# Wider loads and alternating column pairs in the input projection of a decoder layer

## The chip, the cores and the metric

The kernel runs on one core of a Trainium2 chip. The metric is the time of one execution on the device in microseconds (us), taken as the median of several runs; lower is better. One execution was also profiled, and all rows below come from it.

## What is computed

One decoder layer for 256 tokens of width 2048, all in float32. An input projection w_in (2048 x 8208) gives queries, keys, values and output gates for two groups of 8 heads of 128, and 16 scalar gate columns. The first group is an mLSTM, the second a retention. Both mixers' results go through one output projection, then comes a feed-forward network.

```python
h = rmsnorm(x, g_mix_pre[l])
proj = h @ w_in[l]
mq, mk, mv, mo, mi, mf, rq, rk, rv, rg = jnp.split(proj, SPLITS, axis=-1)
qk = jax.nn.silu(causal_dwconv(jnp.concatenate([mq, mk], axis=-1), conv_w[l], conv_b[l]))
...
hm = head_rmsnorm(hm, g_mlstm_head[l]) * jax.nn.sigmoid(mo.astype(f32))
rq_h = rotary(split_heads(rq, N_RET_HEADS).astype(f32), positions)
rk_h = rotary(split_heads(rk, N_RET_HEADS).astype(f32), positions)
hr = retention_chunkwise(rq_h, rk_h, split_heads(rv, N_RET_HEADS).astype(f32))
hr = head_rmsnorm(hr, g_ret_head[l]) * jax.nn.silu(rg.astype(f32))
mix = jnp.concatenate([hm, hr], axis=-1).astype(x.dtype) @ w_out[l]
x = x + rmsnorm(mix, g_mix_post[l])
h = rmsnorm(x, g_ffn_pre[l])
ff = (jax.nn.silu(h @ w_gate[l]) * (h @ w_up[l])) @ w_down[l]
x = x + rmsnorm(ff, g_ffn_post[l])
```

## The kernel before

**Split products.** Each float32 operand is kept as two parts, a rounded one (`hi`) and the rest (`lo`), and a product is made of hi by hi, hi by lo and lo by hi. Weights pass through three stages. SyncE loads 1 MB chunks into `raw` (four chunks, q = 0 to 3). ScalarE copies 1024 columns of it, one **sub**, to `w_hi` (L441). VectorE writes the difference to `w_lo` (L779). `w_hi` and `w_lo` hold four subs (`AHEAD`), so ScalarE copies sub s + 4 as soon as TensorE has ended sub s (`ahead`), and VectorE follows. A chunk of `raw` serves two subs; `load` (L324) fills it again once `lo_done` says that both were used.

**Rounds.** Eight subs are a round. Rounds 0 to 3 make the values, rounds 4 to 15 (`R_IN` to `R_OUT`) the queries, keys and gates: for each of four head groups (two of the mLSTM, two of the retention) a query, a key and a gate round, each of 512 output columns. Rounds 16 to 19 are the output projection, then comes the feed-forward network. In rounds 4 to 15 a round makes two **pairs** (u = 0, 1) of 256 columns. Pair 0 takes subs 0 to 3, pair 1 subs 4 to 7 (`unit_columns`), each sub being 8 products of 512 and 8 of 256 moving columns (`sub_columns`). A load brings 8 rows of 256 columns per partition.

**After a pair.** `unit_at(rnd, s, lag)` says which pair ended `lag` subs ago. With lag 0, ScalarE copies the right half of the pair's two PSUM banks to `right` and VectorE adds the left half to it (`unit_sums`), which frees the banks (`acc_free`). Queries and keys then pass four convolution taps (`convolve`, half 0 at lag 0 and half 1 at lag 1) or the rotation (`rotate`), in the single buffer `new`, and at lag 2 ScalarE writes them to `qT` or `kT`. A gate's sums are scaled, and at lag 1 ScalarE applies the sigmoid (L604); in the retention groups VectorE multiplies at lag 2 by the gate itself (L1086).

**Heads.** The four heads n of a group are worked off from the start of its gate round. `head_at(rnd, s, first)` gives the head whose step falls on sub s. TensorE makes scores at s = 0, 2, 4, 6 and weighted values after s = 1, 3, 5, 7; the latter go to two PSUM banks in turn, so those of head n wait for `y_ready` of head n - 2. VectorE's `head_step` runs first in each step, in this order: `weigh` (head n at s = 2n), `mix` (2n + 6), `head_scaled` (2n + 4, which writes y), variance (2n + 3), reciprocals (2n + 2), `mix_rest` (2n + 8). `mix` (L1055) waits for `gate_sig`, the sigmoid of the head's pair. TensorE turns y of head 0 and 1 after subs 5 and 7, of heads 2 and 3 in the next round (`left_over`). Each engine runs its instructions in the written order.

**The scalar gates.** 16 products with `wg_both` fill bank 3, which is also a bank of pair 1. ScalarE copies parts of it to rows, VectorE combines them in short linked operations (L930 to L947), TensorE turns the result to columns (`gate_columns`), VectorE copies these (L956, L958), and `spread_rows` makes 16 products of 8 rows each for the decay matrices, after sub 0 of round 5.

Of the kernel before, what the change touches and what calls it, by code (L numbers as in the profile page):

```python
# [24 lines left out]
ALU = mybir.AluOpType  # L25
# [90 lines left out]

def unit_at(rnd, s, lag):

    rnd, s = rnd - (lag > s), (s - lag) % 8
    if R_IN <= rnd < R_OUT and s % 4 == 3:  # L120
        return (*divmod(rnd - R_IN, 3), s // 4)
    return None


def hybrid_layer(nc, x, positions, g_mix_pre, w_in, conv_w, conv_b, b_igate, b_fgate, g_mlstm_head,
                 g_ret_head, w_out, g_mix_post, g_ffn_pre, w_gate, w_up, w_down, g_ffn_post,
                 inv_freq, out):
    with ExitStack() as ctx:
# [86 lines left out]

        def acc(pair):
            return bank[:, 2 * pair:2 * pair + 2, :]
# [45 lines left out]
        gates_act = sem("gates_act")  # L263
        gates_dve = sem("gates_dve")
# [53 lines left out]
        def _(sp):  # L318
            def load(rnd, q, src, wait=True):

                if wait:
                    sp.wait_ge(lo_done, 8 * (rnd - 1) + 2 * q + 2)
# [106 lines left out]
        def _(act):  # L429
# [4 lines left out]
            def hi(rnd, s, first=False):  # L434
# [3 lines left out]
                rnd, s = rnd + s // 8, s % 8  # L438
                if not first:
                    act.wait_ge(raw_full[s // 2], 16 * (rnd + 1))  # L440
                act.activation(w_hi[:, s % AHEAD, :], raw[:, s // 2, (s % 2) * SUB:(s % 2 + 1) * SUB],  # L441
                               ACT.Copy).then_inc(hi_done, 1)
# [151 lines left out]
            def mixer_step(rnd, s):  # L594

                ended = unit_at(rnd, s, 0)
# [3 lines left out]
                if ended and ended[1] == 2:  # L600
# [3 lines left out]
                    act.activation(new if group >= 2 else gT[:, two, :], gT[:, two, :], ACT.Sigmoid)\  # L604
                       .then_inc(gate_sig, 1)
                ended = unit_at(rnd, s, 2)
                if ended and ended[1] < 2:
                    group, part, u = ended
                    act.wait_ge(tiles_done, pair_of(group, part, u) + 1)
                    act.activation((qT, kT)[part][:, 2 * u:2 * u + 2, :], new,  # L610
                                   ACT.Silu if group < 2 else ACT.Copy).then_inc(pair_ready, 1)

            def gate_rows():
# [6 lines left out]
                act.wait_ge(gates_dve, 3)  # L620
# [145 lines left out]
        def _(dve):  # L766
# [8 lines left out]
            def lo(rnd, s):  # L775
# [3 lines left out]
                dve.tensor_tensor(w_lo[:, s % AHEAD, :], raw[:, s // 2, (s % 2) * SUB:(s % 2 + 1) * SUB],  # L779
                                  w_hi[:, s % AHEAD, :].bitcast(F32), ALU.subtract).then_inc(lo_done, 1)  # L780
# [147 lines left out]
            for n, p0 in enumerate((0, 32)):  # L928
                z = row(R_Z)[p0:p0 + HEADS]
                link(dve.scalar_tensor_tensor(z, row(R_LEFT_LO)[p0:p0 + HEADS], 1.0,  # L930
                                              row(R_RIGHT_LO)[p0:p0 + HEADS], ALU.mult, ALU.add))
                link(dve.tensor_tensor(z, z, row(R_RIGHT)[p0:p0 + HEADS], ALU.add))
                link(dve.tensor_tensor(z, z, bank[p0:p0 + HEADS, B_GATES, 0:SEQ], ALU.add))
                link(dve.tensor_tensor(z, z, rstd_row[p0:p0 + HEADS, :], ALU.mult))
                gates(dve.tensor_scalar(z, z, vec[p0:p0 + HEADS, 2:3], None, ALU.add), n + 1)
            gates(dve.scalar_tensor_tensor(rowf(R_ABS), rowf(R_Z), -1.0, rowf(R_Z), ALU.mult, ALU.max), 3)
# [135 lines left out]
            def mixer_step(rnd, s):  # L1072
# [9 lines left out]
                ended = unit_at(rnd, s, 2)  # L1082
                if ended and ended[0] >= 2 and ended[1] == 2:
                    group, part, u = ended
# [165 lines left out]
        def _(pe):  # L1250
# [12 lines left out]
            def sub_columns(rnd, s, act_T, pair):  # L1263

                pe.wait_ge(lo_done, 8 * rnd + s + 1)
                slot, quarter = s % AHEAD, s % 4
# [9 lines left out]
            def unit_columns(rnd, unit, event, act_T, before=None, after=None):  # L1276

                pe.wait_ge(acc_free, event + 1)
                for q in range(4):
# [3 lines left out]
                    sub_columns(rnd, s, act_T, unit)  # L1283
# [173 lines left out]
            def gate_units(group, rnd, event):  # L1457
# [11 lines left out]
                for u in range(2):  # L1469
                    unit_columns(rnd, u, event + u, hT, before, after)  # L1470
# [5 lines left out]
            unit_columns(R_IN, 0, event_of(R_IN, 0), hT)  # L1476
            pe.wait_ge(gates_act, 1)
            pe.wait_ge(gates_dve, 2)
            unit_columns(R_IN, 1, event_of(R_IN, 1), hT,
                         after=lambda s: gate_columns() if s == 6 else None)  # L1480
            for u in range(2):
                unit_columns(R_IN + 1, u, event_of(R_IN + 1, u), hT,
                             after=lambda s: spread_rows() if s == 0 else None)
            with pe.Fori(0, 3) as j:
                gate_units(j, 3 * j + gate_round(0), 6 * j + event_of(gate_round(0), 0))
                for n in (1, 2):
                    for u in range(2):
                        unit_columns(3 * j + (gate_round(0) + n), u,
                                     6 * j + event_of(gate_round(0) + n, u), hT,
                                     after=left_over(j) if n == 1 else None)  # L1490
# [121 lines left out]
```

## Time and profile before

| | |
|---|---|
| median of 3 timed runs | 1235.89 us (1235.27 to 1236.32) |
| the profiled execution | 1238.89 us |
| its span, first to last instruction | 1237.2 us |
| granted TensorE clock, mean | 0.996 |
| TensorE busy | 1222.7 us |
| VectorE busy | 717.1 us |
| ScalarE busy | 599.3 us |
| loads of w_in, 63 of 1 MB, issue to landing | 12.8 us (median) |

Rows name an engine (PE is TensorE, DVE VectorE, ACT ScalarE, PEld the weight load of TensorE, SP SyncE), a line of the kernel, what is written and read, and times. Times on a timeline count from the start of the span. Matmuls overlap, so a start-to-start distance tells more of TensorE's pace than one duration does.

### The profile page before, as it was taken

How to read it: one execution, taken by the hardware profiler on the slowest of the kernel's cores; microseconds unless marked ns; L12 is line 12 of the kernel's file. 1: busy time of each engine (PE TensorE's matmuls, PEld its weight loads, DVE VectorE, ACT ScalarE, POOL GpSimd, SP SyncE). 2: the span in 40 equal slices, each digit the busy share in tenths (PEclk: the TensorE clock that was granted, in tenths of full speed). 3: DMA queues.
4: the chain of work that ended last, by engine and by line, in shares of the span. 5: the costliest groups of instructions: out<-in, count | busy, mean ns of one | idle time of the engine just before them, and what ended most of it. 6: DMA issues, size and time to landing. Idle time of an engine off the chain costs nothing.

```text
span 1237.2 us, 15798 instructions
## 1 busy us (share of the span) xinstructions
PE 1222.7 (99%) x5899; PEld 1026.1 (83%) x5899; DVE 717.1 (58%) x923; ACT 599.3 (48%) x789; POOL 14.2 (1%) x35
## 2 busy tenths in 40 slices
PE   8999999999999999999999999999999999999997
PEld 7888888888888888888888888888888888888886
DVE  6656778776777656744554554454455454544544
ACT  5654666574554645644444444444444444443442
POOL 2000100000000000000000000000000000000000
PEclk9999899999999999999999999999999999999999
DMA  8666798867887556465656565555656565556551
GB/s 313 208 145 165 132 213 171 146 166 163 204 179 187 200 178 214 157 193 181 194 180 203 175 198 190 183 192 184 200 173 200 188 220 203 182 192 204 186 188 69
DMA packets 136937, 229.49 MB, mean 185 GB/s; under 512 B 6080, under 2 KB 55488, under 8 KB 136384
## 3 DMA queue, kind: packets, MB, share of 16 engines
q1 hardware_dynamic: 136608, 226.84, 62.8%
q0 software_dynamic: 288, 2.10, 0.4%
q8 instruction: 26, 0.43, 0.1%
q14 instruction: 15, 0.12, 0.0%
HBM read 226.83 MB, written 2.10 MB: 185 GB/s over the span
## 4 chain that ended last, share of the span: by engine, by line
PE 90%; DMA 4%; DVE 3%; ACT 1%; issue 0%; SPq 0%; DVEq 0%; ACTq 0%
PE bank L1252 89%; DMA raw<-in_w_in 4%; DVE w_lo L779 1%; PE bank L1536 1%; DMA resid<-in_x 1%; ACT w_hi L441 1%; PE bank L1257 0%; PE bank L1454 0%; DVE gT L993 0%; ACT L604 0%; DVE h L806 0%; DVE resid L1124 0%; PE bank L1509 0%; DVE pre L966 0%; DVE hT L792 0%
## 5 line engine op out<-in xcount | busy, mean ns | idle before, releaser
L779 DVE TENSOR_TENSOR w_lo<-raw,w_hi 128x1024 fp32r<-128x1024 f32 x420 | 512.9, 1224 | 481.8 <-ACT w_hi L441 481.3
L441 ACT ACTIVATE w_hi<-raw 128x1024 fp32r<-128x1024 f32 x420 | 443.5, 1060 | 569.4 <-PE bank L1252 539.1
L1252 PE MATMUL bank<-w_hi,h2T 128*128 128x512 f32 x1376 | 426.6, 390 | 0.0
L1252 PEld LDWEIGHTS bank<-w_hi,h2T 128*128 128x128 f32 x1376 | 258.3, 188 | 53.4
L1252 PE MATMUL bank<-hT,w_hi 128*128 128x512 f32 x768 | 274.5, 401 | 0.0
L1252 PE MATMUL bank<-w_lo,h2T 128*128 128x512 f32 x688 | 267.7, 389 | 0.0
L1252 PE MATMUL bank<-w_hi,ffT 128*128 128x512 f32 x704 | 217.2, 389 | 0.0
L1252 PE MATMUL bank<-hT,w_lo 128*128 128x256 f32 x768 | 215.4, 280 | 0.0
L1252 PEld LDWEIGHTS bank<-hT,w_hi 128*128 128x128 f32 x768 | 145.5, 190 | 33.8 <-issue 0.2
L1252 PEld LDWEIGHTS bank<-w_hi,ffT 128*128 128x128 f32 x704 | 132.1, 188 | 27.3
L1252 PEld LDWEIGHTS bank<-w_lo,h2T 128*128 128x128 f32 x688 | 129.2, 188 | 26.5
L1252 PEld LDWEIGHTS bank<-hT,w_lo 128*128 128x128 f32 x768 | 146.1, 190 | 0.0
L1252 PE MATMUL bank<-w_lo,ffT 128*128 128x512 f32 x352 | 136.9, 389 | 0.0
L1252 PE MATMUL bank<-w_hi,hT 128*128 128x512 f32 x256 | 81.3, 393 | 0.8 <-DVE w_lo L779 0.8
L1252 PE MATMUL bank<-w_hi,mixT 128*128 128x512 f32 x256 | 80.2, 391 | 0.0
L1252 PEld LDWEIGHTS bank<-w_lo,ffT 128*128 128x128 f32 x352 | 66.1, 188 | 13.8
L1252 PEld LDWEIGHTS bank<-w_hi,hT 128*128 128x128 f32 x256 | 48.0, 188 | 11.3 <-issue 1.2
L1252 PEld LDWEIGHTS bank<-w_hi,mixT 128*128 128x128 f32 x256 | 48.1, 188 | 10.3 <-DVE mixT L1061 0.4
L1252 PE MATMUL bank<-w_lo,hT 128*128 128x512 f32 x128 | 49.9, 390 | 0.0
L1252 PE MATMUL bank<-w_lo,mixT 128*128 128x512 f32 x128 | 49.8, 389 | 0.0
L1252 PEld LDWEIGHTS bank<-w_lo,mixT 128*128 128x128 f32 x128 | 24.0, 188 | 4.9
L1252 PEld LDWEIGHTS bank<-w_lo,hT 128*128 128x128 f32 x128 | 24.1, 188 | 4.7
(176 smaller groups left out, 566.4 us busy)
## 6 DMA issues: line engine op xcount, KB each, us to landing
raw<-in_w_in SPq DMA_DIRECT2D x63, 1024.0 KB, 12.8
raw<-in_w_gate SPq DMA_DIRECT2D x44, 1024.0 KB, 5.1
raw<-in_w_up SPq DMA_DIRECT2D x44, 1024.0 KB, 5.1
raw<-in_w_down SPq DMA_DIRECT2D x44, 1024.0 KB, 5.0
raw<-in_w_out SPq DMA_DIRECT2D x16, 1024.0 KB, 5.0
resid<-in_x SPq DMA_DIRECT2D x2, 1024.0 KB, 7.2
out<-resid SPq DMA_DIRECT2D x8, 256.0 KB, 2.5
raw<-in_w_in SPq DMA_DIRECT2D x2, 512.0 KB, 6.6
```

Of the source, the lines that this page charges most:

```text
L441: act.activation(w_hi[:, s % AHEAD, :], raw[:, s // 2, (s % 2) * SUB:(s % 2 + 1) * SUB], ACT.Copy).then_inc(hi_done, 1)
L779: dve.tensor_tensor(w_lo[:, s % AHEAD, :], raw[:, s // 2, (s % 2) * SUB:(s % 2 + 1) * SUB], w_hi[:, s % AHEAD, :].bitcast(F32), ALU.subtra ...
L1252: return pe.matmul(out_, lhsT, rhs, start=start, stop=stop, skip_group_check=True)
L1536: ins = pe.transpose(bank[:, B_FF + j // 2, c:c + P], ff[:, t, j * P:(j + 1) * P], ident)
```

## The change

Loads of rounds 4 to 15 bring 4 rows of 512 columns per partition, so that each chunk serves both pairs. The order of the subs of a round becomes a table of (pair, chunk). In query and gate rounds (`EVEN_ORDER`) the pairs alternate by two subs: pair 0 ends with sub 5, pair 1 with sub 7. In key rounds (`KEY_ORDER`) pair 0 ends with sub 4. `free_after` gives the count at which a chunk may be overwritten. On ScalarE the activation of a query or key pair moves ahead of the copy of the right half. The gates of the retention groups use one SiLU in place of sigmoid and product. The scalar gates read bank 3 first, and the forget row goes ahead of the input row.

```diff
+EVEN_ORDER = ((0, 0), (0, 1), (1, 0), (1, 1), (0, 2), (0, 3), (1, 2), (1, 3))
+KEY_ORDER = ((0, 0), (0, 1), (1, 0), (0, 2), (0, 3), (1, 1), (1, 2), (1, 3))
+ORDERS = (EVEN_ORDER, KEY_ORDER, EVEN_ORDER)
+FREE = (2, 4, 6, 8)
...
+def free_after(part):
+
+    return [ORDERS[part].index((1, q)) + 1 for q in range(4)]
...
-    if R_IN <= rnd < R_OUT and s % 4 == 3:
-        return (*divmod(rnd - R_IN, 3), s // 4)
+    if R_IN <= rnd < R_OUT:
+        ends = [ORDERS[(rnd - R_IN) % 3].index((u, 3)) for u in range(2)]
+        if s in ends:
+            return (*divmod(rnd - R_IN, 3), ends.index(s))
...
+        def raw_sub(rnd, s):
+
+            if is_wide(rnd):
+                u, q = ORDERS[(rnd - R_IN) % 3][s]
+                return q, raw[:, q, :].rearrange("p (k c) -> p k c", c=512)[:, :, 256 * u:256 * u + 256]
+            return s // 2, raw[:, s // 2, (s % 2) * SUB:(s % 2 + 1) * SUB]
...
-                            col = COL_RET * kind + 512 * half + (part * DH + (q // 2) * 256)
-                            load(6 * kind + 3 * half + (R_IN + n), q,
-                                 in_rows(8 * (q % 2), 8, col, 256))
-            with sp.Fori(0, 4) as g:
+                            col = COL_RET * kind + 512 * half + part * DH
+                            load(6 * kind + 3 * half + (R_IN + n), q, in_rows(4 * q, 4, col, 512),
+                                 free=free_after((n + 2) % 3))
+            for q in range(4):
+                load(R_OUT, q, rows(w_out, 4 * q, 4, 0, 512), free=free_after(2))
+            with sp.Fori(1, 4) as g:
...
+                ended = unit_at(rnd, s, 2)
+                if ended and ended[1] < 2:
+                    group, part, u = ended
+                    act.wait_ge(tiles_done, pair_of(group, part, u) + 1)
+                    act.activation((qT, kT)[part][:, 2 * u:2 * u + 2, :], new,
+                                   ACT.Silu if group < 2 else ACT.Copy).then_inc(pair_ready, 1)
...
-                    act.activation(new if group >= 2 else gT[:, two, :], gT[:, two, :], ACT.Sigmoid)\
+                    act.activation(gT[:, two, :], gT[:, two, :], ACT.Silu if group >= 2 else ACT.Sigmoid)\
                        .then_inc(gate_sig, 1)
...
-            for n, p0 in enumerate((0, 32)):
+            for p0 in (0, 32):
+                dve.tensor_tensor(row(R_Z)[p0:p0 + HEADS], bank[p0:p0 + HEADS, B_GATES, 0:SEQ],
+                                  row(R_RIGHT)[p0:p0 + HEADS], ALU.add).then_inc(gates_left, 1)
+            dve.wait_ge(gates_left, 2)
+            for n, p0 in enumerate((32, 0)):
...
-                    dve.wait_ge(gate_sig, 2 * group + u + 1)
-                    link(dve.tensor_tensor(gT[:, 2 * u:2 * u + 2, :], gT[:, 2 * u:2 * u + 2, :], new,
-                                           ALU.mult))
...
+            def wide_columns(rnd, event, act_T, order, before=None, after=None):
+
+                for s, (u, q) in enumerate(order):
+                    if q == 0:
+                        pe.wait_ge(acc_free, event + (u + 1))
...
+            def gates_consumed(s):
+
+                if s == 2:
+                    pe.wait_ge(gates_act, 1)
+                    pe.wait_ge(gates_left, 2)
```

What stands in a row on ScalarE around the first gate activation of the first group's gate round, before. The first w_hi copy is sub 3's step, the second sub 4's step:

```order
L441 ACTIVATE w_hi<-raw 128x1024 [waits raw_full3,sub_done]
L561 ACTIVATE right<-bank 128x512 [waits acc_free]
L457 ACT_TABLE_LOAD
L457 ACTIVATE stat<-stat 128x2 [waits var_ready]
L588 ACTIVATE stat<-bank 128x2 [waits pv_done]
L441 ACTIVATE w_hi<-raw 128x1024 [waits raw_full0,sub_done]
L604 ACT_TABLE_LOAD
L604 ACTIVATE gT<-gT 128x512 [waits gate_scaled]
```

And there now, where the first w_hi copy is sub 5's step and the second sub 6's step:

```order
L475 ACTIVATE w_hi<-raw 128x1024 [waits raw_full1,sub_done]
L594 ACTIVATE right<-bank 128x512 [waits acc_free]
L490 ACTIVATE stat<-stat 128x2 [waits var_ready]
L621 ACTIVATE stat<-bank 128x2 [waits pv_done]
L475 ACTIVATE w_hi<-raw 128x1024 [waits raw_full0,sub_done]
L643 ACT_TABLE_LOAD
L643 ACTIVATE gT<-gT 128x512 [waits gate_scaled]
```

The gate activation has moved two steps down, behind the copy that waits for sub 6. On VectorE, steps 5 and 6 of the same round, before (`stat` rows are the heads' statistics, L1055 is `mix`, L1047 writes y):

```order
L779 TENSOR_TENSOR w_lo<-raw,w_hi 128x1024 [waits hi_done]
L1021 SCALAR_TENSOR_TENSOR probs<-bank,decay 128x384 [waits pv_done,masked,scores_done]
L1055 SCALAR_TENSOR_TENSOR gT<-bank,columns,gT 128x256 [waits gate_sig,yT_done]
L1041 RECIPROCAL stat<-stat 128x2 [waits sd_ready]
L1042 TENSOR_TENSOR stat<-stat 128x2 [waits dve_step]
L1047 TENSOR_SCALAR y<-bank,stat 128x128 [waits dve_step]
L1047 TENSOR_SCALAR y<-bank,stat 128x128
```

And now, where L1091 is `mix` and L1083 writes y:

```order
L812 TENSOR_TENSOR w_lo<-raw,w_hi 128x1024 [waits hi_done]
L1002 TENSOR_TENSOR gT<-bank,right 128x512 [waits right_ready]
L1005 TENSOR_TENSOR gT<-gT,rstd_row 128x512 [waits acc_free]
L1057 SCALAR_TENSOR_TENSOR probs<-bank,decay 128x384 [waits pv_done,masked,scores_done]
L1091 SCALAR_TENSOR_TENSOR gT<-bank,columns,gT 128x256 [waits gate_sig,yT_done]
L1077 RECIPROCAL stat<-stat 128x2 [waits sd_ready]
L1078 TENSOR_TENSOR stat<-stat 128x2 [waits dve_step]
L1083 TENSOR_SCALAR y<-bank,stat 128x128 [waits dve_step]
L1083 TENSOR_SCALAR y<-bank,stat 128x128
```

The first pair's sums and scaling now stand directly ahead of step 6, and `mix` keeps its place ahead of y. The third place is VectorE's start of the scalar gates, now (before, ten linked operations stood ahead of the absolute value):

```order
L962 TENSOR_TENSOR h0<-bank,h0 8x256 [waits gates_act,rope_ready]
L962 TENSOR_TENSOR h0<-bank,h0 8x256
L968 TENSOR_TENSOR h0<-h0 8x256 [waits gates_left]
L968 TENSOR_TENSOR h0<-h0 8x256 [waits dve_step]
L969 TENSOR_TENSOR h0<-h0,rstd_row 8x256 [waits dve_step]
L970 TENSOR_SCALAR h0<-h0,vec 8x256 [waits dve_step]
L972 SCALAR_TENSOR_TENSOR h0<-h0 8x256 [waits gates_dve]
```

The absolute value (L972) has six operations ahead of it, and the bank is read by the first two.

## Rows read from the trace of the kernel before

**Rows 1.** The page: TensorE's busy time, and the chain by engine.

```profile
PE 1222.7 (99%) x5899; PEld 1026.1 (83%) x5899; DVE 717.1 (58%) x923; ACT 599.3 (48%) x789; POOL 14.2 (1%) x35
...
PE 90%; DMA 4%; DVE 3%; ACT 1%; issue 0%; SPq 0%; DVEq 0%; ACTq 0%
```

**Rows 2.** Waits of TensorE, 106 to 422 us; last row: 410 to 425 us.

```profile
PE bank L1252 <- DVE probs L1021: 1.7, 1, 1.7
PE bank L1252 <- DVE floor L958: 0.8, 1, 0.8
PE bank L1252 <- ACT kT L610: 0.6, 1, 0.6
PE bank L1454 <- DVE y L1047: 0.2, 1, 0.2
...
PEld bank L1454 <- DVE y L1047: 0.5, 1, 0.5
```

**Rows 3.** Windows: busy by engine (count), granted clock, DMA share, GB/s.

```profile
134.50:136.00 1.50, 1.50 (x8) 1.18 (x7) 1.43 (x4) 0.00 (x0) 0.00 (x0) 0.54 0.85 117
136.00:141.00 5.00, 5.00 (x17) 4.32 (x16) 3.60 (x8) 0.07 (x1) 0.00 (x0) 0.50 0.90 97
141.00:143.00 2.00, 2.00 (x11) 1.70 (x11) 0.98 (x1) 1.51 (x2) 0.00 (x0) 0.89 0.61 91
...
304.00:314.00 10.00, 7.79 (x46) 6.40 (x45) 6.98 (x9) 4.16 (x6) 0.00 (x0) 1.00 0.86 230
```

**Rows 4.** Loads: w_in from 30, from 78, w_out; ScalarE's wait (106 to 380).

```profile
raw<-in_w_in SPq DMA_DIRECT2D x7, 1024.0 KB, 7.0
...
DMA to landing us min/median/max: 7.6/13.6/22.4
...
raw<-in_w_out SPq DMA_DIRECT2D x16, 1024.0 KB, 5.0
...
ACT w_hi L441 <- DMA raw<-in_w_in: 23.3, 7, 6.0
```

**Rows 5.** ScalarE's timeline, first gate round: start, duration, what, idle before.

```profile
175.47 1.06 ACT L441 ACTIVATE w_hi<-raw 128x1024 fp32r<-128x1024 f32 x1 [0.98 <-PE bank L1252]
176.55 1.28 ACT L604 ACT_TABLE_LOAD   x1
177.84 0.63 ACT L604 ACTIVATE gT<-gT 128x512 f32<-128x512 f32 x1
...
182.56 1.06 ACT L441 ACTIVATE w_hi<-raw 128x1024 fp32r<-128x1024 f32 x1 [0.73 <-PE bank L1252]
...
185.34 1.06 ACT L441 ACTIVATE w_hi<-raw 128x1024 fp32r<-128x1024 f32 x1 [0.49 <-PE bank L1252]
...
189.00 1.06 ACT L441 ACTIVATE w_hi<-raw 128x1024 fp32r<-128x1024 f32 x1 [1.97 <-PE bank L1252]
```

**Rows 6.** Timeline at the scalar gates (VectorE) and the row spread (TensorE).

```profile
107.96 0.40 DVE L930 SCALAR_TENSOR_TENSOR h<-h 8x256 f32<-8x256 f32 x1
...
131.95 0.28 PE L1252 MATMUL bank<-hT,w_lo 128*128 128x256 f32 x1
133.00 2.47 PE L1252 MATMUL bank<-neg_m,sel_r 8*128 8x256 f32 x16 [0.77 <-DVE floor L958]
```

**Rows 7.** VectorE's timeline in the first gate round; L1086 in all.

```profile
181.90 0.48 DVE L1055 SCALAR_TENSOR_TENSOR gT<-bank,columns,gT 128x256 f32<-128x256 f32 x1
...
182.68 0.61 DVE L1047 TENSOR_SCALAR y<-bank,stat 128x128 f32<-128x128 f32 x2
...
196.05 0.61 DVE L1047 TENSOR_SCALAR y<-bank,stat 128x128 f32<-128x128 f32 x2
...
L1086 DVE TENSOR_TENSOR gT<-gT,pre x4: 684/684/686, 330.6 to 418.4; 128x512 f32<-128x512 f32 x4
```

**Rows 8.** TensorE's timeline, first group: weighted values and turned y of head 3.

```profile
185.14 0.83 PE L1252 MATMUL bank<-v_sb,probs 128*128 x6
...
197.35 0.38 PE L1454 MATMUL bank<-columns,y 128*128 128x128 f32 x2
```

More of the change, by code:

```diff
@@ L318, in _, with load @@
         def _(sp):
-            def load(rnd, q, src, wait=True):
+            def load(rnd, q, src, wait=True, free=FREE):
                 if wait:
-                    sp.wait_ge(lo_done, 8 * (rnd - 1) + 2 * q + 2)
+                    sp.wait_ge(lo_done, 8 * (rnd - 1) + free[q])
                 k = src.shape[1]
@@ L438, in hi @@
                 rnd, s = rnd + s // 8, s % 8
+                chunk, src = raw_sub(rnd, s)
                 if not first:
-                    act.wait_ge(raw_full[s // 2], 16 * (rnd + 1))
-                act.activation(w_hi[:, s % AHEAD, :], raw[:, s // 2, (s % 2) * SUB:(s % 2 + 1) * SUB],
-                               ACT.Copy).then_inc(hi_done, 1)
+                    act.wait_ge(raw_full[chunk], 16 * (rnd + 1))
+                act.activation(part_of(w_hi, rnd, s), src, ACT.Copy).then_inc(hi_done, 1)
             def early_hi(s):
@@ L778, in lo @@
                 dve.wait_ge(hi_done, 8 * rnd + s + 1)
-                dve.tensor_tensor(w_lo[:, s % AHEAD, :], raw[:, s // 2, (s % 2) * SUB:(s % 2 + 1) * SUB],
-                                  w_hi[:, s % AHEAD, :].bitcast(F32), ALU.subtract).then_inc(lo_done, 1)
+                dve.tensor_tensor(part_of(w_lo, rnd, s), raw_sub(rnd, s)[1],
+                                  part_of(w_hi, rnd, s).bitcast(F32), ALU.subtract).then_inc(lo_done, 1)
             def early_lo(s):
@@ L927, in _ @@
             dve.wait_ge(gates_act, 1)
-            for n, p0 in enumerate((0, 32)):
+            for p0 in (0, 32):
[3 more added lines that the diff above has]
+            for n, p0 in enumerate((32, 0)):
                 z = row(R_Z)[p0:p0 + HEADS]
[L930 to L933, printed above, removed]
+                for lower in (R_LEFT_LO, R_RIGHT_LO):
+                    link(dve.tensor_tensor(z, z, row(lower)[p0:p0 + HEADS], ALU.add))
                 link(dve.tensor_tensor(z, z, rstd_row[p0:p0 + HEADS, :], ALU.mult))
-                gates(dve.tensor_scalar(z, z, vec[p0:p0 + HEADS, 2:3], None, ALU.add), n + 1)
-            gates(dve.scalar_tensor_tensor(rowf(R_ABS), rowf(R_Z), -1.0, rowf(R_Z), ALU.mult, ALU.max), 3)
+                gates(dve.tensor_scalar(z, z, vec[p0:p0 + HEADS, 2:3], None, ALU.add), 2 * n + 1)
+                if n == 0:
+                    gates(dve.scalar_tensor_tensor(rowf(R_ABS), rowf(R_Z), -1.0, rowf(R_Z), ALU.mult, ALU.max), 2)
             link(dve.memset(rowf(R_ONES), 1.0))
@@ L1261, in transposed, with sub_columns @@
                     ins.then_inc(xT_done, 1)
[L1263 removed]
+            def sub_columns(rnd, s, act_T, pair, quarter):
                 pe.wait_ge(lo_done, 8 * rnd + s + 1)
[L1266 removed]
+                slot = s % AHEAD
                 for c in range(2):
@@ L1282, in unit_columns @@
                         before(s)
-                    sub_columns(rnd, s, act_T, unit)
+                    sub_columns(rnd, s, act_T, unit, q)
+                    if after:
+                        after(s)
+            def wide_columns(rnd, event, act_T, order, before=None, after=None):
+                for s, (u, q) in enumerate(order):
+                    if q == 0:
+                        pe.wait_ge(acc_free, event + (u + 1))
+                    if before:
+                        before(s)
+                    sub_columns(rnd, s, act_T, u, q)
                     if after:
```

39 lines of the change are left out of this document (15 added, 24 removed).

## The prediction

> **What bounds the kernel now.** I read the page first: TensorE is busy 99% of the span, and 90% of the chain that ended last is TensorE [rows 1]. So only three things move the time: products added or removed, clock lost, and idle time of TensorE. The change adds and removes no product. Therefore the next view is TensorE's waits in the input projection (106 to 422 us): 1.7, 0.8, 0.6 and 0.2 us, four waits in all [rows 2]. The clock by windows shows the rest: it is 0.54 from 134.5 us and 0.50 from 136, and comes back within the window from 141 (0.89) [rows 3]. Time at the half level is about 6.8 us (92% of 1.5 us, 5 us, and 22% of 2 us), so 3.4 us are lost. All that the change can win is thus 3.3 us of waits, 0.2 us in the last gate round (below), and 3.4 us of clock: 6.9 us of 1236. Anything larger has to come as a loss.
>
> **Part 1: wider loads.** 48 loads of 1 KB runs become 48 loads of 2 KB runs of the same 1 MB. Now they land in 13.6 us in the median, 22.4 us at most, while the 512-column loads of w_out, of the very shape that w_in's now get, land in 5.0 us, and the 1024-column loads of w_in itself in 7.0 us [rows 4]. I take 5 to 9 us, nearest to these two, and keep 13.6 us as the upper bound. ScalarE waited 23.3 us for such loads in this stage, 7 times [rows 4]; three of TensorE's waits hang on that: the key activation (0.6 us), the weighted scores (1.7 us) and the turned head (0.2 us) [rows 2]. They go: -2.5 us. Another of this kind, a turned head in the last gate round (0.5 us of the weight load's wait [rows 2], of which the matmul row shows 0.2 us), also goes, since the SiLU now needs no product on VectorE (0.69 us [rows 7]) ahead of it: -0.2 us.
>
> The Trainium skill (Perfetto Trace Analysis, DMA Optimizations) says that transfers under 2 KB carry much overhead per transfer and that batching can improve throughput dramatically. Taken as the main effect it would promise far more, but here TensorE waits 2.7 us in all behind those loads, so the trace caps the gain whatever the bandwidth does.
>
> The other side of it: a chunk is now free later. In the key round chunk 1 is released after the sixth sub and wanted by the second of the next round: three subs instead of six. A sub is 2.78 us (the two w_hi copies at 182.56 and 185.34 [rows 5]), and the counts stand for a copy that follows its release by 3 x 2.78 plus 0.5 us, 8.8 us. TensorE uses the sub three later, less 2.3 us for w_hi and w_lo, so it has 6.0 us more, 14.8 us. The upper bound of 13.6 us fits for TensorE, not for ScalarE. I cost it at nothing; the cover is those 6.0 us.
>
> **Part 2: the gates' start and the row spread.** TensorE's wait for the gates' bank moves from the fifth to the third sub, 5.6 us after the round's start at 106.8. VectorE starts on them at 107.96, and an operation there takes 0.40 us [rows 6]; two additions free the bank at 108.8, against 112.3. No cost. The forget row then comes first: its absolute value follows 6 operations instead of 10, 4 x 0.44 = 1.8 us earlier, and with it everything down to the columns. The first query pair ends two subs later, but still ahead of the columns, so VectorE has the same work before them. I follow it by durations: sub 5 ends at 106.8 + 6 x 2.78 = 123.5, the copy behind it at 124.7, then on VectorE w_lo to 125.9, sums, norm and taps 2.9, w_lo 1.1, taps 1.6, columns 0.2: 131.8 us, where TensorE got them shortly before 133.00 now [rows 6]. TensorE is there at 132.2 (last product's start 131.95 plus 0.28). Its wait of 0.8 us [rows 2, 6] goes: -0.8 us. The cover is 0.4 us thin; if it fails, up to 0.8 us stays.
>
> Whether the clock still falls is open. It fell about 2.3 us after the dense products ended, within the 16 products of 8 rows, which took 2.5 us themselves [rows 3, 6]. These stay; only 0.8 us of idle time goes. Bounds: 0 and -3.4 us. I take 0, since the spread alone is as long as the stretch after which the clock fell.
>
> **Part 3: the gate round, where the change costs.** Before, the first pair of a gate round ends with sub 3 and ScalarE makes its sigmoid behind the w_hi copy of sub 4: copy 175.47, table 176.55, sigmoid 177.84 to 178.47, so 3.00 us from copy to end [rows 5]. VectorE multiplies with it in step 6 (L1055), without a wait, and in the same step makes y of head 1: 181.90 to 183.29, 1.39 us [rows 7]. TensorE wants y of head 1 (its PSUM bank) before the fourth weighted product, at 185.14 [rows 8], 1.85 us later. Now the pair ends with sub 5, the sigmoid stands in ScalarE's step 6, behind a copy that waits for sub 6, and VectorE's step 6 still multiplies first. So the multiplication waits: copy 182.56 [rows 5] + 3.00 = 185.56, + 1.39 = 186.95, + 0.1 for two hand-overs = 187.05, against 185.14. TensorE stands still for 1.9 us. Nothing gives it back, since TensorE has no other idle time. Queued behind the waiting multiplication are y, the reciprocals of head 2, and w_lo of sub 10; behind these ScalarE's squares and the next two copies. w_lo of sub 10 ends at 188.5 and is used from 193.5, covered. The turned heads are not quite: y of head 2 is then ready at about 193.6 where TensorE, itself 1.9 us later, comes at 193.5; y of head 3, 7.7 us (189.00 to 196.66) behind its step's copy, at 199.5 against 199.4 [rows 5, 7, 8]. That is 0 to 0.8 us more, I take 0.15. There are four gate rounds: 4 x (1.9 + 0.15) = +8.2 us.
>
> One price inside this differs from the Trainium skill (ScalarE: Activation LUTs, What ACT_TABLE_LOAD costs): 1.28 us for the load plus 1.38 us of drain for each switch. The row agrees with the load; the activation starts 0.01 us after it ends (176.55 + 1.28, then 177.84 [rows 5]). The measurement decides; with the page's drain the sum would be 4 x 1.4 us higher.
>
> **The rest of the pairs.** The second pair now ends two subs (5.6 us) before its banks are wanted again, instead of four. In a query round ScalarE must first take the first pair's activation: taps end about 2.8 us after the last sub, activation 0.6, copy of the right half 0.6, sum 0.7: 4.75 us. Covered by 0.8 us; nothing. Copies and differences read raw in four pieces of 256: the same sizes, no cost.
>
> **Sum**, against this execution's own 1238.9 us (span 1237.2): -2.7 - 0.8 + 8.2 = +4.7 us, 1243.6 us. The median of the timed runs lies 3.0 us under the profiled one, so 1235.9 + 4.7 = **1240.6 us**.
>
> **Rivals.** (a) The clock holds through the spread. For it: 0.8 us less without dense products. Against: the 2.5 us of thin ones. It takes off 3.4 us: 1237.2 us, 0.1% slower. (b) The faster side: the sigmoid does not reach TensorE. The place is the wait of L1055's product for gate_sig in step 6; it decides at 1.85 us between y of head 1 and the weighted product [rows 7, 8]. If the sigmoid were ready by 184, through an order of the engines that I misread, only the gains are left: 1235.9 - 3.5 = 1232.4 us, or 1229.0 with the clock kept. Against it: in the order both engines' rows stand as told, and the copy before the table load waits for sub 6. (c) The clock falls at the new 1.9 us gaps as well. Before, the wait of 1.7 us [rows 2] left it at 1.00 (the window from 304) [rows 3]; the new gap is longer. One fall costs the 3.4 us above: 1244.0 us with one, 1254.2 us with four. (d) Loads stay at 13 us or more and the short spans after key rounds reach ScalarE's copies in the gate rounds: the three waits of part 1 stay, +2.7, and about 1 us more: 1244.3 us. (e) That the loads are not wider is out: the order shows 128x4x512.
>
> **Chances.** Forecast 0.46, (a) 0.27, (b) 0.10, (c) 0.12, (d) 0.05. About 0.2% (2.5 us) is what a measurement of this kernel can tell from no change. Faster by more: (b), 0.10. Within: (a), 0.27. Slower: forecast, (c) and (d), 0.63. The range takes in the forecast with its bounds (0.8 us for the columns, up to 0.6 us a gate round), (a), (d) and (c) with one fall: 1234.5 to 1246.0 us; outside are (b) and most of the rest of (c).
>
> **What would show it.** In the profile after: a wait of TensorE for y or, at the fourth weighted product, of about 1.9 us, four times; VectorE's gate product waiting for the sigmoid's line on ScalarE four times, about 3 us each; no wait for the floor columns; w_in landings at 5 to 9 us and no ScalarE wait for them; the clock by windows near 134 us. The prediction is wrong if TensorE's waits in the gate rounds sum to under 4 us, if the clock falls more than once, or if the loads land no sooner.

## The result, and the profile after

| | before | after |
|---|---|---|
| median of 7 timed runs | 1235.89 us (1235.27 to 1237.51) | 1244.73 us (1242.16 to 1249.26) |
| ratio | | 1.0074 (95%: 1.0056 to 1.0093) |
| the profiled execution | 1238.89 us | 1242.16 us |
| its span | 1237.2 us | 1240.5 us |

The change makes the kernel 0.74% slower: 8.8 us, where 4.7 us were forecast. The page of the profile after still shows a kernel bound by TensorE [rows 1], now with less of it busy:

```profile
PE 1219.0 (98%) x5899; PEld 1023.9 (83%) x5899; DVE 715.0 (58%) x919; ACT 600.4 (48%) x789; POOL 13.2 (1%) x35
```

The waits from 106 to 422 us (engine, line, who was waited for: total, times, longest), which answer to [rows 2] and the last row of [rows 4]:

```profile
DVE gT L1091 <- ACT gT L643: 13.4, 4, 3.4
...
PE bank L1282 <- DVE y L1083: 7.9, 4, 2.0
ACT w_hi L475 <- DMA raw<-in_w_in: 3.8, 2, 2.0
...
PE bank L1282 <- ACT kT L633: 2.1, 2, 1.8
```

The three waits behind loads and the one for the floor columns are gone. In their place TensorE waits 7.9 us for `y`, four times, and 2.1 us for `kT`, twice. The first of the four, on the timelines of ScalarE, VectorE and TensorE (start, duration, what, idle time before), to be held against [rows 5, 7, 8]:

```profile
177.90 0.16 ACT L621 ACTIVATE stat<-bank 128x2 f32<-128x2 f32 x1
180.73 1.06 ACT L475 ACTIVATE w_hi<-raw 128x1024 fp32r<-128x1024 f32 x1 [2.67 <-PE bank L1282]
181.81 1.28 ACT L643 ACT_TABLE_LOAD   x1
183.10 0.63 ACT L643 ACTIVATE gT<-gT 128x512 f32<-128x512 f32 x1
```

```profile
183.84 0.48 DVE L1091 SCALAR_TENSOR_TENSOR gT<-bank,columns,gT 128x256 f32<-128x256 f32 x1 [3.37 <-ACT gT L643]
...
184.63 0.61 DVE L1083 TENSOR_SCALAR y<-bank,stat 128x128 f32<-128x128 f32 x2
```

```profile
185.49 0.93 PE L1282 MATMUL bank<-v_sb,probs 128*128 x6 [1.97 <-DVE y L1083]
```

ScalarE idles for 2.67 us until sub 6 has ended, then copies, loads the table, and makes the sigmoid; VectorE stands 3.37 us before the gate product, with `y` queued behind it, and TensorE 1.97 us before the weighted values. The other new wait is at the start of the first group's gate round (TensorE, then ScalarE, then VectorE):

```profile
156.00 0.92 PE L1282 MATMUL bank<-qT,kT 128*128 128x256 f32 x4 [1.78 <-ACT kT L633]
```

```profile
152.52 1.28 ACT L633 ACT_TABLE_LOAD   x1
155.32 0.63 ACT L633 ACTIVATE kT<-pre 128x512 f32<-128x512 f32 x1 [1.52 <-DVE pre L1029]
```

```profile
152.47 1.23 DVE L812 TENSOR_TENSOR w_lo<-raw,w_hi 128x1024 fp32r<-128x1024 f32 x1
153.61 0.88 DVE L1029 SCALAR_TENSOR_TENSOR gT<-pre,columns,gT 128x256 f32<-128x256 f32 x2
154.40 0.88 DVE L1029 SCALAR_TENSOR_TENSOR pre<-pre,columns,gT 128x256 f32<-128x256 f32 x2
```

The key pair that now ends with sub 4 of the key round instead of sub 3 passes its taps behind a `w_lo`, and the scores want it at 154.2 us. At the row spread (timeline of TensorE, against [rows 6]) there is no idle time, and the clock, by a window as in [rows 3], stays at the full level through the whole stretch:

```profile
132.07 2.17 PE L1282 MATMUL bank<-neg_m,sel_r 8*128 8x256 f32 x16
```

```profile
106.00:425.00 319.00, 308.96 (x1803) 270.57 (x1802) 236.62 (x417) 188.07 (x305) 5.81 (x17) 1.00 0.65 168
```

The loads of w_in from 78 us on (against [rows 4]) land in 9.0 us instead of 13.6:

```profile
DMA to landing us min/median/max: 5.9/9.0/14.2
```

**The account.** The profiled execution before lost 3.4 us to the clock at 134 us, the one after nothing there. So, held at the full clock, the two stand at 1235.5 and 1242.2 us: +6.7 us. The rows give +7.9 (`y`) + 2.1 (`kT`) - 0.8 (floor) - 2.5 (waits behind loads) = +6.7 us. That it closes so well is in part luck. A wait costs more than the idle time listed for it: from the first `w_hi` product of a round to that of the next, the four gate rounds last 118.8 us here and 109.7 us in e11 below, which has no waits for `y`. That is 9.0 us for a listed 7.9. Small differences in the pace of the products (see e1) stand against it.

The medians differ by 8.8 us, 2.1 us more. The median after lies 2.6 us above its profiled execution, that of before 0.4 us above the 1235.5 us worked out for the full clock. The mean granted clock is 0.998 in the profiled execution after and 0.993 to 0.997 in the four slowest timed runs. The experiments bear on what that is.

### The profile page after: what moved, and what is told of

The parts are those of the page before. It is cut to its first block, busy times and chain, and to the rows that moved or that the text cites. A ratio compares the mean times of both kernels' runs of the same rounds, so it can differ in the third digit from the quotient of the medians.

```text
span 1240.5 us, 15775 instructions
## 1 busy us (share of the span) xinstructions
PE 1219.0 (98%) x5899; PEld 1023.9 (83%) x5899; DVE 715.0 (58%) x919; ACT 600.4 (48%) x789; POOL 13.2 (1%) x35
## 4 chain that ended last, share of the span: by engine, by line
PE 94%; DVE 2%; ACT 2%; DMA 1%; issue 0%; SPq 0%; DVEq 0%
PE bank L1282 93%; PE bank L1577 1%; DMA resid<-in_x 1%; ACT w_hi L475 1%; DVE w_lo L812 1%; ACT L643 0%; PE bank L1287 0%; PE bank L1495 0%; DVE gT L1029 0%; ACT gT L643 0%; DVE y L1083 0%; ACT decay L587 0%; DVE h L839 0%; DVE resid L1154 0%; PE bank L1550 0%
## 5 line engine op out<-in xcount | busy, mean ns | idle before, releaser
L1282 PE MATMUL bank<-hT,w_hi 128*128 128x512 f32 x768 | 271.2, 397 | 0.0
L1282 PEld LDWEIGHTS bank<-w_lo,ffT 128*128 128x128 f32 x352 | 66.1, 188 | 13.6
```

The costliest lines, as they stand in the source:

```text
L1282: return pe.matmul(out_, lhsT, rhs, start=start, stop=stop, skip_group_check=True)
```

## The experiments

Each kernel ran in five rounds beside the kernel before, whose medians were 1236.09 us (first four rows below), 1236.48 us (next four) and 1236.13 us (last two).

| kernel | median (range), us | ratio to before (95%) |
|---|---|---|
| e1_y_first | 1241.49 (1240.27 to 1244.14) | 1.0050 (1.0036 to 1.0064) |
| e3_late_sigmoid | 1244.65 (1243.39 to 1251.81) | 1.0081 (1.0059 to 1.0103) |
| e4_narrow | 1246.21 (1244.72 to 1249.36) | 1.0086 (1.0072 to 1.0101) |
| e8_filled | 1243.08 (1242.18 to 1245.15) | 1.0060 (1.0047 to 1.0073) |
| e2_gate_early | 1237.11 (1234.70 to 1238.36) | 0.9997 (0.9986 to 1.0008) |
| e9_both | 1235.02 (1233.47 to 1237.61) | 0.9987 (0.9976 to 0.9997) |
| e5_input_row_first | 1246.68 (1244.20 to 1249.33) | 1.0077 (1.0057 to 1.0097) |
| e7_gates_only | 1234.37 (1233.24 to 1240.31) | 0.9981 (0.9964 to 0.9997) |
| e11_sig_ahead | 1233.72 (1233.14 to 1235.43) | 0.9980 (0.9972 to 0.9989) |
| e12_sig_and_taps | 1232.14 (1231.43 to 1233.60) | 0.9967 (0.9956 to 0.9978) |

The theory: the late sigmoid makes the four waits for `y` and with them most of the loss. The rivals: the loss comes from the loads or the order of subs itself, or from the clock.

### The late sigmoid in the old kernel (e3)

The kernel before, with the first gate pair's activation two steps later; retention gates use one SiLU, as after.

```diff
-                ended = unit_at(rnd, s, 1)
-                if ended and ended[1] == 2:
+                ended = unit_at(rnd, s, 3 if s == 6 else 1)
+                if ended and ended[1] == 2 and s != 4:
...
```

> The kernel before with its own loads, its own order of pairs and its own scalar gates, but the activation of the first gate pair is put two steps later on ScalarE, behind the copy of sub 10 (retention gates with one SiLU, as in the change, because the second product would stand in the way). Theory: TensorE waits for y four times, 1.9 us each, so +7.7 us, less 0.2 us for the SiLU: 1243 us where the clock holds, and a spread of several us above it, as in the changed kernel. Rival 1 (loads or interleaving): within 1 us of the kernel before, 1236 us.

Its waits, and windows around one place:

```profile
DVE gT L1055 <- ACT gT L604: 18.7, 4, 4.7
PE bank L1246 <- DVE y L1047: 8.0, 4, 2.0
```

```profile
262.00:263.00 1.00, 0.81 (x7) 0.82 (x8) 0.97 (x2) 0.73 (x4) 0.00 (x0) 1.00 0.67 188
263.00:266.50 3.50, 3.50 (x15) 3.02 (x13) 2.40 (x5) 3.47 (x8) 0.00 (x0) 0.52 0.38 89
```

The same four waits, 8.0 us, without any of the change's loads or orders, and 8.6 us more time than before. The mechanism stands. The windows show something more: directly behind the second of the four gaps the granted clock is at 1.2 GHz for about 3.4 us, which costs 1.7 us. The clock is not all that varies: the slowest run (1251.81 us) has the same mean clock, 0.996, as the three runs between 1243.4 and 1244.8 us. What it lost is not known.

### y ahead of the gate product (e1)

```diff
-                for step, first in ((weigh, 0), (mix, 6), (head_scaled, 4), (head_variance, 3),
+                for step, first in ((weigh, 0), (head_scaled, 4), (mix, 6), (head_variance, 3),
```

> The changed kernel, but VectorE's head step writes y (L1083) ahead of the product with the gate (L1091); nothing else moves. Theory (the late gate activation holds y of head 1, and through it TensorE): the four waits of about 2.0 us before the fourth weighted product go, and at most 0.3 us each is left before the turned head behind it, since that needs the gate product of head 0. The wait for keys (2.1 us) stays. With no 2 us gaps left the clock should fall no more there, so the runs lie close together: about 1235 us in the median, spread under 2 us. Rival 1 (wider loads or the interleaved pairs themselves cost): still 1240 us or more. Rival 2 (the clock falls for another reason, such as the row spread): the median falls by 7 us only and the spread of 7 us stays.

It missed by 6 us, and by its own terms it spoke for rival 1 (loads or pairs, 1240 us or more), which e3 speaks against and e11 below refutes. TensorE no longer waits for `y` before the weighted values, but for the gate product before the turned heads, at 106 to 425 us:

```profile
PE bank L1495 <- DVE gT L1091: 2.9, 9, 0.5
...
PE bank L1282 <- ACT kT L633: 2.0, 2, 1.8
```

Of 7.9 us 5.0 are saved by the waits, yet the span is only 1.2 us shorter (1239.3 us). The starts of the rounds say where the rest is. The four gate rounds are 6.8 us shorter in all. The stretches behind them, in which heads 2 and 3 are turned (three query rounds and the output projection), are 4.3 us longer, and the three key rounds from the second group on 1.1 us longer. Two things make that up. A late turned head costs more than its listed wait. In the changed kernel it starts 0.12 us after the product before it, here 0.55 us, for a listed 0.27:

```profile
191.91 0.28 PE L1282 MATMUL bank<-hT,w_lo 128*128 128x256 f32 x1
192.03 0.38 PE L1495 MATMUL bank<-columns,y 128*128 128x128 f32 x2
```

```profile
190.41 0.28 PE L1282 MATMUL bank<-hT,w_lo 128*128 128x256 f32 x1
190.96 0.41 PE L1495 MATMUL bank<-columns,y 128*128 128x128 f32 x2 [0.27 <-DVE gT L1091]
```

Over all turned heads these distances are 4.8 us longer than in the changed kernel, for 2.9 us of listed waits. The other is the pace of the products. A sub that nothing interrupts takes 2.77 us in some stretches and 2.83 us in others, all at the full clock: of 41 such subs 35 are slow here and 5 in the changed kernel, which is 1.7 us. Windows of 20 us of nearly the same stretch, in the changed kernel and here, show it as 118 products against 115:

```profile
281.00:301.00 20.00, 20.00 (x118) 1.00 0.71 171
```

```profile
281.00:301.00 20.00, 20.00 (x115) 1.00 0.70 173
```

e11, which differs from the changed kernel in one instruction of ScalarE, also has 115 there, and 15 slow subs in all. What sets the pace was not found.

### Narrow loads under the new order (e4)

The changed kernel with loads of 8 rows of 256 columns. The order and the ends of the pairs are kept; the counts at which a chunk may be overwritten change with the layout.

```diff
-                            col = COL_RET * kind + 512 * half + part * DH
-                            load(6 * kind + 3 * half + (R_IN + n), q, in_rows(4 * q, 4, col, 512),
+                            col = COL_RET * kind + 512 * half + (part * DH + (q % 2) * 256)
+                            load(6 * kind + 3 * half + (R_IN + n), q, in_rows(8 * (q // 2), 8, col, 256),
...
```

> The changed kernel with its order of pairs, its activations and its scalar gates, but with loads of 8 rows of 256 columns as before, laid out so that a chunk serves two subs of one pair. Theory: the y waits stay (7.9 us); loads take 13 us again, so ScalarE waits for them some 20 us in all, and the 0.6 to 2.5 us that TensorE lost through them come back: 1243 to 1247 us. Rival 1 (the wide loads are what costs, through the shorter spans for a chunk): 1238 us or less. If the wide loads gave nothing: as the changed kernel within 1 us, with no more waits of TensorE in its profile.

```profile
ACT w_hi L476 <- DMA raw<-in_w_in: 11.2, 4, 3.7
PE bank L1283 <- DVE y L1084: 8.8, 4, 2.9
...
PE bank L1283 <- ACT kT L634: 2.1, 2, 1.8
```

The loads of w_in land in 11.8 us instead of 9.0 (medians of the two pages), and ScalarE waits 11.2 us for them, where some 20 were expected. One wait for `y` grows to 2.9 us, in the round in which ScalarE waits 3.19 us for a load at 259 us. The waits account for 0.9 us more than in the changed kernel. The other 3.4 us of this profile are two falls of the clock, one at the row spread (135 us) and one behind the wait of 2.9 us (264.8 us). The median lies 1.5 us above the changed kernel's, with intervals of the ratios that overlap, so what the wide loads are worth under this order is not settled by the times. The loss itself stays with narrow loads: it is not theirs.

### The gaps filled with work (e8)

The changed kernel plus 8 products of 512 columns, extra work into bank 0, before the fourth weighted values of each gate round.

```diff
+                        if s == 7:
+                            pe.wait_ge(acc_free, event + 3)
+                            for _ in range(8):
+                                mm(bank[:, 0, :], hT[:, 0, 0:P], hT[:, 0, :], True, True)
```

> The changed kernel with eight products of 512 columns added on TensorE in each gate round between sub 7 and the fourth weighted product, about 1.8 us, in the time in which it stands still; their result is overwritten. Theory (the clock falls in the idle gaps, in some executions): the lowest time stays at 1242 us, because the gap is only filled, and the spread goes: median within 1 us of the lowest, and the mean granted clock the same in all runs. Rival 2 (the clock falls elsewhere): the spread of 7 us stays and the median stays at 1244 to 1245 us.

```profile
PE bank L1282 <- ACT kT L633: 2.0, 2, 1.8
PE bank L1282 <- DVE y L1083: 0.2, 1, 0.2
```

```profile
156.00:157.00 1.00, 0.78 (x4) 0.72 (x5) 0.64 (x1) 1.00 (x2) 0.00 (x0) 0.87 0.86 207
157.00:160.00 3.00, 3.00 (x11) 2.61 (x11) 2.78 (x4) 0.60 (x2) 0.00 (x0) 0.50 0.89 183
```

The idle time became work of the same length, and the fastest run is the same to 0.02 us (1242.18). But the runs spread over 3.0 us instead of 7.1, and the median is 1.65 us lower. These are six runs against seven, and the intervals of the two ratios overlap, so this supports, and does not prove, that the clock falling behind the gaps lifts the changed kernel's median over its fastest run. The fall that this profile holds stands right behind the one long gap that was not filled, that for `kT` (1.8 us). The mean clock was expected to be the same in all runs; it is 0.996 to 0.999.

### The gate pair ends one sub sooner (e2)

```diff
-ORDERS = (EVEN_ORDER, KEY_ORDER, EVEN_ORDER)
+ORDERS = (EVEN_ORDER, KEY_ORDER, KEY_ORDER)
...
-                wide_columns(rnd, event, hT, EVEN_ORDER, before, after)
+                wide_columns(rnd, event, hT, KEY_ORDER, before, after)
```

> The changed kernel with one table entry changed: gate rounds run in KEY_ORDER, so that the first gate pair ends with sub 4 instead of sub 5 and its sigmoid stands one step earlier on ScalarE. Theory (the sigmoid's place sets the four 2.0 us waits for y): the gate product on VectorE finds the sigmoid ready (at about 181.3 us in the first gate round, where it is wanted at 181.9), TensorE's waits for y go from 7.9 us to under 1 us, without the waits of the turned heads that the other order of the head step had; span 1240.5 - 7.9 = 1232.6 to 1234 us, and no clock falls at gate gaps. Rival (a second link, such as VectorE's load with the sums of both pairs, is late next): over 3 us of waits stay at the weighted or turned products, and the span is 1237 us or more.

```profile
ACT w_hi L475 <- DMA raw<-in_w_in: 14.8, 7, 3.0
...
PE bank L1282 <- ACT kT L633: 2.1, 2, 1.8
DVE gT L1091 <- ACT gT L643: 1.3, 4, 0.3
PE bank L1282 <- DVE probs L1057: 1.2, 1, 1.2
```

All 7.9 us for `y` are gone, and the time is that of the kernel before. The span, 1235.4 us, is over the 1232.6 to 1234 us expected: 1240.5 - 7.9 = 1232.6 us, plus 1.2 us for `probs` and 1.7 us for one fall of the clock at the row spread, makes 1235.5. The price is visible: chunk 1 is free later in the gate rounds too, ScalarE waits 14.8 us for loads instead of 3.8, and once that reaches TensorE (1.2 us).

### The keys' taps first (e9)

As e2, and in VectorE's loop, for step 5 of a key round:

```diff
+                    taps_first = (rnd - R_IN) % 3 == 1 and s == 5
+                    if taps_first:
+                        mixer_step(rnd, s)
                     lo(rnd, s + AHEAD)
-                    mixer_step(rnd, s)
+                    if not taps_first:
+                        mixer_step(rnd, s)
```

> The kernel with gate rounds in KEY_ORDER, and in step 5 of a key round VectorE finishes the first pair's taps before it makes w_lo of the sub ahead. Theory (TensorE's 2.1 us of waits for kT at the start of the gate rounds hang on VectorE's taps, which end at 155.28 us behind a w_lo of 1.14 us): the key activation ends 1.1 us sooner, the waits of 1.78 and 0.37 us shrink to 0.7 and 0 us; span 1.5 us under that of the kernel with gate rounds in KEY_ORDER alone. Rival (w_lo of sub 9 becomes late, or the activation is held by ScalarE's table load): the same waits of about 2 us stay, or show at w_lo instead.

```profile
PE bank L1286 <- DVE probs L1057: 1.8, 1, 1.8
...
PE bank L1286 <- ACT kT L633: 0.6, 1, 0.6
```

The waits for `kT` fall from 2.1 to 0.6 us, as told, and the span from 1235.4 to 1234.0 us. The wait behind the loads stays (1.8 us). The clock fell in both profiles at the row spread, though nothing waits there; in this one:

```profile
134.50:137.90 3.40, 3.40 (x13) 2.92 (x12) 3.37 (x8) 1.06 (x1) 0.00 (x0) 0.52 0.67 175
```

### The scalar gates (e5, e7)

e5 is the changed kernel with the input row first again and the absolute value behind both rows; e7 is the kernel before with only the scalar gates' new code.

```diff
-            for n, p0 in enumerate((32, 0)):
+            for n, p0 in enumerate((0, 32)):
...
```

> The changed kernel with the scalar gates in the old order of rows: input row first, and the absolute value behind both rows. Theory (the forget row first brings the columns 1.8 us sooner and takes the 0.8 us wait at the row spread away): a wait of TensorE of 0.5 to 1.8 us for floor or cols stands at 131 to 133 us again, span 1241 to 1242.5 us where the clock holds; a clock fall at the spread, if the idle time there decides it, adds up to 3.4 us. Rival (the columns were no longer late because the first query pair ends later, whatever the row order): no wait, the same time as the changed kernel, 1242 to 1245 us.

> The kernel before with only the scalar gates' part of the change: bank 3 read first, forget row first, absolute value after six operations. Theory: the columns are ready 1.8 us sooner, the wait of 0.8 us for the floor columns before the row spread goes, nothing else moves: 0.8 us less, so about 1235 us, and 1233.1 us where the clock holds. If the fall of the clock at 134 us in the profile before came from that 0.8 us of idle time, it is absent here in every run; if it comes from the 16 products of 8 rows alone, it still shows in some runs (3.4 us more). Rival: the columns are late behind the first query pair's taps, not behind the gates' operations, and nothing changes.

The waits of e5:

```profile
PE bank L1282 <- ACT kT L633: 3.1, 2, 2.8
...
PE bank L1282 <- DVE floor L994: 0.2, 1, 0.2
```

The row order alone is worth 0.2 us at the spread, less than the 0.5 expected, and 1.0 us at `kT`: the decay exponentials start later on ScalarE and hold up the copy of the key pair's right half (from 149.48 us, against 148.16). The profile's span is 1246.5 us, 6.0 us above the changed kernel's: 1.2 us of waits, and three falls of the clock (at 158.0, 188.7 and 267.2 us) of 1.7 us each, each beginning 0.3 to 1.2 us after the end of a wait, those for `kT` and for the first two `y`. In e7 the columns are copied at 130.78 and 130.86 us, against 132.61 and 132.69 us before, and the spread follows without a wait:

```profile
130.78 0.17 DVE L960 COPY a_col<-bank 128x16 f32<-128x16 f32 x1
130.86 0.16 DVE L962 COPY floor<-bank 128x16 f32<-128x16 f32 x1
```

```profile
132.14 1.58 PE L1256 MATMUL bank<-neg_m,sel_r 8*128 8x256 f32 x11
```

So this part alone is worth 1.8 us on the columns and the 0.8 us of wait; the median is 2.1 us lower, with an interval of the ratio that means 0.4 to 4.5 us. Its profiled execution (1240.31 us) also shows how much the old loads vary from one execution to the next:

```profile
PE bank L1256 <- DVE probs L1025: 5.3, 2, 2.8
```

```profile
164.00:168.00 4.00, 4.00 (x16) 3.45 (x15) 3.54 (x9) 0.69 (x2) 0.00 (x0) 0.57 0.72 192
```

Two waits behind loads of up to 2.8 us, and behind each a clock fall. That the slow executions of the kernel before (up to 1244.98 us, mean clock 0.992) come from the same is likely and not shown.

### The sigmoid ahead of the copy (e11, e12)

The order of subs and loads stays that of the changed kernel. Only ScalarE's activation of the first gate pair moves ahead of the copy that waits for sub 6; e12 adds e9's change of VectorE's taps. The call is moved out of ScalarE's `mixer_step` for the first pair alone:

```diff
                     head_step(rnd, s)
+                    gate_pair(rnd, s, 0)
                     ahead(rnd, s)
                     mixer_step(rnd, s)
```

> The changed kernel, all its sub orders kept; only on ScalarE the first gate pair's activation moves from behind the w_hi copy of step 6 to ahead of it. Theory (the copy that waits for sub 6, and not the pair's later end by itself, makes the sigmoid late): ScalarE loads the table at about 178.2 us while it had idled, the sigmoid runs from about 180.2 to 180.8 us instead of 183.2 to 183.8, the copy still starts at 180.8, the gate product waits under 0.4 us, and TensorE's 7.9 us of waits for y are gone: span 1240.5 - 7.9 = about 1232.6 us, median 1233.5 to 1236. The two waits for kT (2.1 us) stay. Rival (the pair's end with sub 5 is itself too late, since VectorE's scaling must come first): the waits for y stay above 1 us each, span 1237 us or more.

> As the one before, and in step 5 of a key round VectorE finishes the first pair's taps before w_lo of the sub ahead. Theory: both new waits of the change are gone or small (y 0, kT 0.6 us), loads land in 9 us and are not late because the gate rounds keep EVEN_ORDER: TensorE's waits from 106 to 422 us sum to under 1.5 us, span about 1231 us where the clock holds, median 1231.5 to 1234.5, at least 0.15% under the kernel before. Rival (the pace of the products between the waits, which is not the same in all traces, or clock falls at the row spread take it back): waits as told, but the time 1235 us or more.

ScalarE's timeline in e11, against the four rows of after above, and VectorE's gate product:

```profile
177.97 1.28 ACT L647 ACT_TABLE_LOAD   x1
179.93 0.63 ACT L647 ACTIVATE gT<-gT 128x512 f32<-128x512 f32 x1 [0.68 <-DVE gT L1010]
180.62 1.06 ACT L475 ACTIVATE w_hi<-raw 128x1024 fp32r<-128x1024 f32 x1
```

```profile
180.68 0.48 DVE L1096 SCALAR_TENSOR_TENSOR gT<-bank,columns,gT 128x256 f32<-128x256 f32 x1 [0.31 <-ACT gT L647]
```

Table load and sigmoid now lie in time in which ScalarE was idle, and the copy starts when it did. The span is 1231.9 us, 8.6 us less, by a move of one instruction, and there is no fall of the clock before the last microseconds. In e12 the waits of TensorE in the whole stretch are one:

```profile
PE bank L1291 <- ACT kT L633: 0.6, 1, 0.6
```

e12 is 0.33% faster than the kernel before, with an interval from 0.22 to 0.44%, and the fastest that was measured; its eight runs spread over 2.2 us.

## Why the prediction held, point by point

- **In short.** The direction, the place and the mechanism of the main term were right. The size was half of what came: +4.7 us forecast, +8.8 measured, inside the stated range. Of the 4.1 us that lack, 2.0 are a step that was wrong (the first key pair) and 2.1 the clock.
- **What bounds it.** TensorE's waits carried the result at full clock: +6.7 us in four terms, all read as waits of that engine.
- **Part 1, -2.7 us.** Right for 2.5 us of waits. The further 0.2 us was read wrongly: the matmul row's 0.2 us in [rows 2] is the turned head at 270.8 us, already counted, and the one at 420.6 us has only the weight load's 0.5. That one went too; what it gave is not in the account. The landing fell to 9.0 us, the upper end of the 5 to 9 taken. The cover for chunk 1 was enough for TensorE, which waits for no load. ScalarE was to wait for none and waits twice, 3.8 us in all. The Trainium skill (Perfetto Trace Analysis, DMA Optimizations) expects larger transfers to move data better: by e4 and the changed kernel it does (11.8 against 9.0 us), and the profiles give TensorE 0.9 us less waiting for it under the new order.
- **Part 2, -0.8 us.** Right. The columns were ready at 131.44 us, for 131.8 forecast.
- **Part 3, +8.2 us.** The four main waits were forecast at 1.9 us each, 7.6 us, and came at 7.9. The gate product's wait was forecast at 3 us and came at 3.4. The 0.15 us a round for turned heads did not come. e3 and e11 show the cause from both sides: the late sigmoid alone makes the loss in the old kernel, and its earlier place alone takes it out of the new.
- **The rest of the pairs: the step that failed.** I followed the second pair of a round and the query rounds, and wrote "nothing". The first key pair was not followed. It ends one sub later, its activation was due one sub later, and the scores of head 0 did not move: +2.1 us that the sum lacks. With it, the sum would have been +6.8, against +6.7 measured at full clock; that it fits so closely is again in part luck, see the account. e9 and e12 show the cause: with the pair's taps ahead of `w_lo` the wait falls to 0.6 us.
- **The clock.** Rival (c), given 0.12, is not a rival but an addition. The four waits stand in the profiled execution; in others, by e3, e5 and e8, the clock also falls behind one or more of the gaps. The median lies 2.6 us and the slowest run 7.1 us above the fastest. Two of the seven runs have a mean clock of 0.994 and 0.993, which against 0.998 is an estimated 5 to 6 us, about three falls: by the prediction's own sign (the clock falls more than once) it fails in these. A fall was priced at 3.4 us, from the one that stood in the profile before; those behind single gaps cost 1.7 us each. The same rows led to the wrong step in the other direction, that a gap of 1.7 us leaves the clock alone: it did so in the one execution that was profiled. The window shown for it in [rows 3] even ends at 314 us, 0.7 us behind the wait, while a fall in e5 began 1.2 us behind its wait. The trace of before holds none there, so the reading was right by luck.
- **Rival (a).** At the spread the clock held in the profile after, but it fell there in e2, e4 and e9, without any wait, so the 0.8 us of idle time does not decide it. The rival's price was wrong as well: it took 3.4 us off a median that lies 3 us under the execution with the fall, so most timed runs of before are likely to have held the clock already. Of 59 later runs 43 have a mean clock of 0.997 or more, against 0.996 in the profile.
- **Rival (b), the faster side.** Its place and its price were right. It needed the sigmoid before 184 us, which the change did not bring and e11 did: 1233.7 us with the waits for `kT` left in, where 1232.4 had been worked out.

## What to carry to other kernels

When the order of work on the bound engine changes, list for each result its new time of readiness and its unmoved time of use, for every kind of round, and not only for those that the change names: the missing one here cost 2.1 us. On an engine with a strict order, an instruction behind a wait for something it doesn't need is late by that wait; moving the sigmoid ahead of a copy took 8.6 us off the span, while swapping its consumers only moved the wait. Read a single profile's clock as one draw: price idle gaps of the bound engine with the chance of a clock fall on top. When a variant is slower than its waits explain, as e1 was, measure the rounds from start to start.

## What the runs showed of the hardware

- Idle gaps of TensorE of about 2 us are followed in some executions by 3.4 us at 1.2 GHz instead of 2.4 (e3, e8; 0.50 in the windows), in others not: the six gaps of the profile after, 0.4 to 2.0 us, left it at 1.00. With four gaps filled the spread shrank from 7.1 us (seven runs) to 3.0 us (six).
- The clock also fell without a listed wait: in e2, e4 and e9 it goes to 1.2 GHz for 3.4 us at 134.6 to 135.4 us, behind 16 products of 8 rows that took 2.2 us from 132.2 us on (e2). In the profiles of after, e1, e3, e5, e7, e8, e11 and e12 the same products are followed by none.
- A late product costs TensorE more than its listed idle time: 0.55 us from start to start instead of 0.12 for a listed 0.27 (e1), and 9.0 us over the four gate rounds for a listed 7.9 (after against e11).
- The same products, at the same granted clock, run at more than one pace: 118 or 115 in 20 us, a sub in 2.77 or 2.83 us. The two kernels of the windows differ in the order of VectorE's work only, and e11, which has the slow pace there too, in that of ScalarE's. The cause stays open. Over the input projection it amounts to 1.7 us (e1), as much as a wait.
- A load of 1 MB of w_in lands in 13.6 us (median) before and in 9.0 us after (5.0 us for w_out's, which have the same shape [rows 4]); later freeing of its buffer, not its landing, then made ScalarE wait 14.8 us in e2.
- A table load that stands before a wait runs during it: in e11 it ended at 179.25 us and the activation started at 179.93 us, when its data came.
